# Probabilities copied by SyncE and turned as float32r, the largest transfers issued by GpSimd, in an encoder block with attention and routed experts

## The reference, cut to what matters

```python
def one_block(qblk):                      # 128 queries against all 512 keys
    sc = jnp.einsum('bqkgd,bskd->bkgqs', qblk, k).astype(jnp.float32) * scale
    p = jax.nn.softmax(sc, axis=-1).astype(v.dtype)
    return jnp.einsum('bkgqs,bskd->bqkgd', p, v)
...
o = jnp.concatenate([rms_norm(oa, p['out_norm_a']), rms_norm(ob, p['out_norm_b'])], axis=-1)
x = x + jnp.einsum('bse,ed->bsd', o, p['w_o'])
h2 = rms_norm(x, p['norm_ffn'])
x = x + expert_choice_moe(h2, p['w_router'], p['w_gate'], p['w_up'], p['w_down'])
```

## Time and profile before

| | us |
|---|---|
| median of three runs | 1082.65 (1082.18 to 1087.85) |
| the profiled execution, its own time | 1086.1 |
| its span, first to last instruction | 1083.7 |
| mean granted TensorE clock | 0.986 |
| TensorE busy | 1044.8 (96%) |
| VectorE busy | 886.0 (82%) |
| ScalarE busy | 775.3 (72%) |
| GpSimd busy | 423.3 (39%) |

### The profile page before, as it was taken

One profiled execution on the slowest core, in us unless ns is written; L12 is line 12 of the kernel. 1 busy time (PEld: TensorE's weight loads), 2 busy tenths in 40 slices (PEclk: granted clock), 3 DMA queues, 4 the chain that ended last, 5 costly groups with the idle time before them and its releaser, 6 DMA issues.

```text
span 1083.7 us, 16970 instructions
## 1 busy us (share of the span) xinstructions
PE 1044.8 (96%) x5689; PEld 896.7 (83%) x5689; DVE 886.0 (82%) x1147; ACT 775.3 (72%) x1095; POOL 423.3 (39%) x394
## 2 busy tenths in 40 slices
PE   8999999999999999998699999999999999999995
PEld 7999978999889987887578888888888888888884
DVE  6787669989999843338899999999999999999991
ACT  7655569888998843344577877877878878788771
POOL 2466576111358502334524432344323444234101
PEclk9999999999999999999799999999999999999998
DMA  8232050010211348741799999999999999999982
GB/s 305 79 116 102 1 197 1 2 41 20 98 41 40 98 109 263 225 164 79 235 417 378 398 400 400 400 421 400 401 400 400 413 408 401 400 400 406 415 310 39
DMA packets 77936, 266.05 MB, mean 245 GB/s; under 512 B 11249, under 2 KB 13516, under 8 KB 77628
## 3 DMA queue, kind: packets, MB, share of 16 engines
q1 hardware_dynamic: 69776, 239.68, 56.9%
q0 software_dynamic: 8048, 25.68, 8.3%
q10 hardware_dynamic: 60, 0.01, 0.0%
HBM read 239.07 MB, written 26.28 MB: 245 GB/s over the span
## 4 chain that ended last, share of the span: by engine, by line
PE 48%; DVE 2%; DMA 1%; issue 1%; ACT 0%; POOLq 0%; POOL 0%; DVEq 0%; ACTq 0%
PE ps L2003 10%; PE ps L2005 10%; PE ps L2004 10%; PE ps L2017 5%; PE ps L2019 5%; PE ps L2018 5%; PE ps L1980 1%; DMA xe<-h,idxT 1%; DMA out<-y,give 1%; DVE lo L2171 0%; DVE idx L1776 0%; DVE affT L1785 0%; DVE gates L1771 0%; ACT hi L2093 0%; POOLq L2274 0%
## 5 line engine op out<-in xcount | busy, mean ns | idle before, releaser
L2171 DVE TENSOR_TENSOR lo<-raw,hi 128x2048 fp32r<-128x2048 f32 x191 | 430.0, 2285 | 32.3 <-ACT hi L2093 32.0
L2093 ACT ACTIVATE hi<-raw 128x2048 fp32r<-128x2048 f32 x192 | 364.6, 1918 | 70.0 <-PE ps L2005 57.3
L2003 PE MATMUL ps<-hi,xehi 128*128 128x512 f32 x480 | 188.3, 392 | 1.3 <-DVE h L2193 1.0
L2005 PE MATMUL ps<-hi,xelo 128*128 128x512 f32 x480 | 186.9, 389 | 0.0
L2004 PE MATMUL ps<-lo,xehi 128*128 128x512 f32 x480 | 186.8, 389 | 0.0
L1939 POOL DMA_INDIRECT xe<-h,take x60 | 111.1, 1851 | 25.1 <-issue 13.7
L2003 PEld LDWEIGHTS ps<-hi,xehi 128*128 128x128 f32 x480 | 90.1, 188 | 20.2 <-issue 1.4
L2005 PEld LDWEIGHTS ps<-hi,xelo 128*128 128x128 f32 x480 | 90.1, 188 | 18.8
L2004 PEld LDWEIGHTS ps<-lo,xehi 128*128 128x128 f32 x480 | 90.2, 188 | 18.1
L1934 POOL COPY take<-idx 128x4 uint32 (+1 forms) x15 | 29.0, 1930 | 193.7 <-DVE xt L2187 187.4
L1361 DVE TENSOR_TENSOR probTlo<-ps,probThi 128x512 fp32r<-128x512 f32 x128 | 87.8, 686 | 12.1 <-ACT probThi L1318 10.0
(11 more groups left out here) (302 smaller groups left out, 2192.3 us busy)
## 6 DMA issues: line engine op xcount, KB each, us to landing
raw<-in_w_down SPq DMA_DIRECT2D x64, 1024.0 KB, 10.0
raw<-in_w_gate SPq DMA_DIRECT2D x60, 1024.0 KB, 9.7
raw<-in_w_up SPq DMA_DIRECT2D x60, 1024.0 KB, 9.3
w_raw<-in_w_in SPq DMA_DIRECT2D x8, 592.0 KB, 9.0
x<-in_x SPq DMA_DIRECT2D x8, 512.0 KB, 3.7
woraw<-in_w_o SPq DMA_DIRECT2D x4, 1024.0 KB, 5.1
o<-attention_out SPq DMA_DIRECT2D x8, 512.0 KB, 4.4
xr<-in_x SPq DMA_DIRECT2D x8, 512.0 KB, 7.0
```

What stands on the lines that cost most here:

```text
L2003: pe.matmul(ps[:, dst[n], :], rowhi[:, c, :], hi[w][:, cols], start=c == 0, stop=False)
L2005: last = pe.matmul(ps[:, dst[n], :], rowlo[:, c, :], hi[w][:, cols], start=False, stop=c == KD - 1)
L2093: act.activation(hi[s][:], raw[s][:], ACT.Copy).then_inc(hi_done, 1)
L2171: dve.tensor_tensor(lo[s][:], raw[s][:], hi[s][:].bitcast(F32), ALU.subtract).then_inc(lo_done, 1)
```

## The change

From the seventh unit on (`DIRECT = 6`), SyncE copies each unit's probabilities by DMA, SBUF to SBUF, 256 KB each, into one of three new tiles `turn`, when the exponential is done and the turns of three units ago are too. The turns read the copy. They are float32 for u % 4 = 0 and float32r for the other three of four units (and float32 for the first six units); in- and output are the same bytes seen as the other type, and the identity is written as float32r. An exponential now waits for the copy that read its buffer three units ago. All steps of attention behind the exponential come one step later (9 instead of 8 steps of drain); pairs of value products now fall on odd steps, and in them the four turns stand one by one ahead of the four "lo" products. The stores of finished heads and the loads of `w_o` are issued by GpSimd, at fixed places of its loop over key heads; SyncE issues the first row block's heads after unit 94's copy, its residual after the loop, and then what it issued before, without the stores. Some buffers change place.

```diff
@@ attend: names @@
-    STEPS = 8
+    STEPS = 9
+    turn = att["turn"]
+    turn_loaded = project_signals["w_loaded"][0:len(turn)]
+    DIRECT = 6
+    def loaded(v):
+        return turn_loaded[v % 3], 16 * (v // 3)
+    def exp_read(v):
+        return (pt_ready, v + 1) if v < DIRECT else loaded(v)
@@ attend: SyncE @@
     def sync_program(sp, route_first, route_second, route_rest):
-        for h0, h1 in O_PARTS:
-            store_heads(0, h0, h1)
-        sp.wait_ge(o_stored, 16 * len(O_PARTS))
-        for i in range(KD // 2):
-            if i >= 2:
-                sp.wait_ge(wo_lo, 2 * (i - 1))
-            sp.dma_start(wo["raw"][:, 2 * (i % 2):2 * (i % 2) + 2, :],
-                         a["w_o"].rearrange("(k p) n -> p k n", p=P)[:, 2 * i:2 * i + 2, :]).then_inc(wo_loaded, 16)
-        route_first(sp)
-        for h0, h1 in O_PARTS[:-1]:
-            store_heads(1, h0, h1)
+        for v in range(DIRECT, NU):
+            sp.wait_ge(exp_done, v + 1)
+            sp.wait_ge(pt_ready, v - 2)
+            sp.dma_start(turn[v % 3][:], att["p"][v % 3][:]).then_inc(turn_loaded[v % 3], 16)
+            if v == NU // 2 + 30:
+                route_first(sp)
         route_second(sp)
-        store_heads(1, *O_PARTS[-1])
         route_rest(sp)
@@ attend: GpSimd @@
+        stores = {QH + 5: (0, 0), HEADS: (0, 1), HEADS + GROUP: (0, 2), HEADS + QH + 4: (1, 0), HEADS + QH + 6: (1, 1)}
...
+            if g in stores:
+                s, part = stores[g]
+                store_heads(pool, s, *O_PARTS[part])
+                if (s, part) == (0, len(O_PARTS) - 1):
+                    pool.wait_ge(o_stored, 16 * len(O_PARTS))
+                    load_output_weights(0)
+                    load_output_weights(1)
             for i in split_after.get(g, ()):
                 split_output_weights(pool, i)
+                if i in (1, 3):
+                    load_output_weights((i + 3) // 2)
+        store_heads(pool, SETS - 1, *O_PARTS[-1])
@@ attend: TensorE @@
         def transpose_prob(u, i):
             if i == 0:
-                pe.wait_ge(exp_done, u + 1)
+                if u < DIRECT:
+                    pe.wait_ge(exp_done, u + 1)
+                else:
+                    pe.wait_ge(*loaded(u))
...
-            turned = pe.transpose(ps[:, T_BANKS[u % 2], cols], att["p"][u % 3][:, cols], k["ident"][:])
+            rows = att["p"] if u < DIRECT else turn
+            as_type = F32 if u < DIRECT or u % TS == 0 else F32R
+            turned = pe.transpose(ps[:, T_BANKS[u % 2], cols].bitcast(as_type), rows[u % 3][:, cols].bitcast(as_type),
+                                  k["ident"][:].bitcast(as_type))
...
-        def values(m):
+        def values(m, between):
...
                 else:
+                    if between is not None:
+                        transpose_prob(between, i)
                     pe.matmul(ps[0:VD, OT_BANK, cols], v[:, i, 0, :], ptlo[m % 2][:, i, :], start=False, stop=False)
...
-            pair = (u - 6) // 2 if u >= 6 and u % 2 == 0 and (u - 6) // 2 < PAIRS else None
-            turned = u - 3 if 0 <= u - 3 < NU else None
-            output = (u - 11) // TS if u >= 11 and (u - 11) % TS == 0 else None
+            pair = (u - 7) // 2 if u >= 7 and u % 2 == 1 and (u - 7) // 2 < PAIRS else None
+            turned = u - 4 if 0 <= u - 4 < NU else None
+            output = (u - 12) // TS if u >= 12 and (u - 12) % TS == 0 else None
@@ attend: ScalarE (and VectorE's steps, each one later in the same way) @@
                 if v >= 3:
-                    act.wait_ge(pt_ready, v - 2)
+                    act.wait_ge(*exp_read(v - 3))
...
-            if 0 <= u - 3 < NU:
-                v = u - 3
+            if 0 <= u - 4 < NU:
+                v = u - 4
@@ route: SyncE @@
     def sync_first(sp):
-        sp.wait_ge(wo_lo, KD)
-        load_rows(sp, 0)
+        sp.wait_ge(o_stored, 16 * len(O_PARTS))
+        load_attended(sp, 0)
     def sync_second(sp):
+        sp.wait_ge(wo_lo, KD)
+        load_residual(sp, 0)
         sp.wait_ge(score_ready, UNITS)
         load_rows(sp, 1)
```

More of the change, by code:

```diff
@@ L252, in build @@
         att["ot"] = bm("ot", [P, SEQ])
+        att["turn"] = [bm("turn0", [P, SEQ])]
         assert bm.at <= w_in_end, (bm.at, w_in_end)
@@ L262, in build @@
         wo["small"] = om("smallo", [P, 128])
-        wo["wr"] = om("wr", [P, KD, EXPERTS])
         wo["aff"] = [om(f"aff{i}", [P, 64]) for i in range(2)]
+        att["turn"] += [om(f"turn{i}", [P, SEQ]) for i in (1, 2)]
         assert om.at <= end
         om3 = Map(temps_at)
-        wo["o"], wo["x"] = [om2("o0", [P, D])], [om2("xr0", [P, D])]
+        om2.at += D * 4
+        wo["x"] = [om2("xr0", [P, D])]
         wo["othi"], wo["otlo"] = [om2("othi0", [P, KD, P], F32R)], [om2("otlo0", [P, KD, P], F32R)]
@@ L274, in build @@
         assert om2.at <= w_in_end
+        wo["o"] = [None]
         for i in (1, 2):
@@ L280, in build @@
         wo["gffn"] = om3("gffn", [P, D])
+        wo["wr"] = om3("wr", [P, KD, EXPERTS])
+        wo["o"][0] = om3("o0", [P, D])
         assert om3.at <= weights_at, (om3.at - weights_at)
@@ L474, in gpsimd_program @@
         steps.wait()
-        pool.affine_select(out=k["ident"][:], in_=k["ident"][:], compare_op=ALU.not_equal, fill=1.0,
+        pool.affine_select(out=k["ident"][:].bitcast(F32R), in_=k["ident"][:], compare_op=ALU.not_equal, fill=1.0,
                            base=0, pattern=[[-1, P]], channel_multiplier=1).then_inc(ident_ready, 1)
@@ L1112, in split_output_weights, with load_output_weights @@
             pool.tensor_tensor(wo["lo"][:, i, :], raw, wo["hi"][:, i, :].bitcast(F32), ALU.subtract).then_inc(wo_lo, 1)
+        def load_output_weights(i):
+            if i >= 2:
+                pool.wait_ge(wo_lo, 2 * (i - 1))
+            pool.dma_start(wo["raw"][:, 2 * (i % 2):2 * (i % 2) + 2, :],
+                           a["w_o"].rearrange("(k p) n -> p k n", p=P)[:, 2 * i:2 * i + 2, :]).then_inc(wo_loaded, 16)
+        stores = {QH + 5: (0, 0), HEADS: (0, 1), HEADS + GROUP: (0, 2), HEADS + QH + 4: (1, 0), HEADS + QH + 6: (1, 1)}
         split_after = {HEADS + GROUP: (0, 1), HEADS + QH: (2, 3), HEADS + QH + 1: (4,), HEADS + QH + 2: (5,),
@@ L1239, in tensor_program @@
                 scores(u)
-            pair = (u - 6) // 2 if u >= 6 and u % 2 == 0 and (u - 6) // 2 < PAIRS else None
-            turned = u - 3 if 0 <= u - 3 < NU else None
-            output = (u - 11) // TS if u >= 11 and (u - 11) % TS == 0 else None
-            for i in range(TS):
-                if output is not None:
-                    turn_output(output, i)
-                if turned is not None:
-                    transpose_prob(turned, i)
-            if pair is not None:
-                values(pair)
+            pair = (u - 7) // 2 if u >= 7 and u % 2 == 1 and (u - 7) // 2 < PAIRS else None
+            turned = u - 4 if 0 <= u - 4 < NU else None
+            output = (u - 12) // TS if u >= 12 and (u - 12) % TS == 0 else None
+            if pair is not None:
+                values(pair, turned)
+            else:
+                for i in range(TS):
+                    if output is not None:
+                        turn_output(output, i)
+                    if turned is not None:
+                        transpose_prob(turned, i)
             if u == NU - 3:
@@ L1295, in scalar_program @@
         for u in range(NU + STEPS):
-            if u >= 9 and (u - 9) % TS == 0:
-                g = (u - 9) // TS
+            if u >= 10 and (u - 10) % TS == 0:
+                g = (u - 10) // TS
                 act.wait_ge(pv_done, TS // 2 * (g + 1))
@@ L1356, in vector_program @@
         for u in range(NU + STEPS):
-            if 0 <= u - 4 < NU:
-                v = u - 4
+            if 0 <= u - 5 < NU:
+                v = u - 5
                 dve.wait_ge(pthi_done, v + 1)
@@ L1368, in vector_program @@
                 prepare(kind, g)
-            if u >= 11 and (u - 11) % TS == 0:
-                g = (u - 11) // TS
+            if u >= 12 and (u - 12) % TS == 0:
+                g = (u - 12) // TS
                 h = g % HEADS
```

27 lines of the change are left out of this document (16 added, 11 removed).

## The result

| | before | after |
|---|---|---|
| median of the runs | 1083.67 us (20 runs, 1082.10 to 1087.85) | 1090.98 us (20 runs, 1085.35 to 1097.54) |
| ratio, 95% interval | | 1.0063 (1.0049 to 1.0078) |
| profiled execution, span | 1086.1, 1083.7 | 1090.85, 1088.5 |
| last maximum of attention starts | 381.13 | 388.53 |
| first product of the experts starts | 531.42 | 536.05 |

What follows compares the result with a forecast made beforehand. TensorE alone was taken to bound the latent heads, with VectorE right behind at 96% in the grouped heads. Terms -5.9 - 3.3 + 1.0 + 1.3 - 3.7 = -10.6 us took the profiled 1086.1 to 1075.5, median 1072.0; range 1065 to 1083.

Steps and rivals of the forecast that it cites:

- step 7: Attention: copies that meet a 0.5 or 1 MB transfer are late, +1.0 us, bounds 0 and 8.
- Steps 1, 2 and 4: TensorE, latent heads: interleaved turns save 0.40 us a group, lone turns lose 0.02; over 16 groups -5.9 us.
- step 1: Odd units' turns between "lo" products: a pair takes 0.17 us against 0.225, saving 0.40 us a group.
- rival 2: Float32r turns load as quickly as float32 turns: another 0.2 us a latent group, -3.2, giving 1069; chance 0.12.
- Step 5: Grouped heads: VectorE at 96% leaves at most 4%; 14 settled groups at 0.24 us, -3.3.
- Step 6: SyncE's 256 KB copies: 2.3 us plus 0.3 for semaphores, hidden under 3.6 us of cover with 1 to spare.
- rival 3: The copy becomes the bound, TensorE waiting ahead of each unit's first turn; +12, 1095 us; chance 0.15.
- Step 8: Drain of attention: the last turns wait for the last copy to land, +1.3 us (0.5 to 2.5).
- Step 9: GpSimd's stream takes six stores and four loads; the work queued behind has slack, so it costs nothing.
- Step 10: After attention: earlier small loads remove TensorE's wait for the third row block and its lower clock, 2.2 + 1.5 = -3.7 us.
- steps 1 to 4: TensorE's savings in latent heads, with u % 4 = 0 staying float32 for nothing: 0.37 us a group, -5.9 in all.

Runs made afterwards that it cites:

- E1: Changed kernel with its four w_o loads cut to 32 of 1024 columns, the output product using other weights: 1076.06 us, ratio 0.9930 to the kernel before.
- E4: Changed kernel with every turn as float32, copies and all else kept: 1097.91 us, ratio 1.0130 to the kernel before.
- E7: E1's kernel with all four turns of a unit ahead of the pair's products in the grouped heads: 1076.28 us, ratio 0.9926 to the kernel before.
- E9: Changed kernel with w_o loads still issued by GpSimd, but held until units 74, 78, 91 and 101, as in E5: 1085.29 us, ratio 1.0021.
- E12: E11's kernel with five more units (53, 54, 66, 67, 118, at the stores) turned straight from the probabilities: 1078.21 us, ratio 0.9953.
- E6: Changed kernel with each 1 MB w_o load as four 256 KB pieces by SyncE, two behind each of two copies: 1082.37 us, ratio 0.9987.
- E10: E5's kernel with the turns of units with u % 4 = 0 as float32r too: 1082.54 us, ratio 1.0005 to the kernel before.
- E13: Kernel before with only the small loads (norm_ffn, router's weights) issued ahead of the last heads' store: 1082.44 us beside 1083.64, ratio 0.9988.
- E16: E13's kernel, unchanged, profiled for one more execution: 1082.30 us.
- E8: Changed kernel without any copy, all turns float32 straight from the probabilities, which get a fourth buffer: 1081.59 us, ratio 0.9983 to the kernel before.
- E3: Changed kernel with the four whole w_o loads issued by SyncE behind the copies of units 78, 82, 98 and 107: 1090.69 us, ratio 1.0073.
- E5: Changed kernel with the four whole w_o loads issued by SyncE behind the copies of units 74, 78, 91 and 101: 1081.94 us, ratio 0.9984.
- E17: Changed kernel, unchanged, profiled for a second execution: 1084.55 us beside one execution of the kernel before of 1083.97.
- E11: E5's kernel with sixteen units beside the loads turned as float32 straight from the probabilities, no copy, fourth buffer: 1077.37 us, ratio 0.9949.
- E14: Kernel before, unchanged, profiled a second time, one execution: 1090.19 us.
- E15: Kernel before, unchanged, profiled a third time, one execution: 1083.41 us.

## Why the prediction was wrong

The sum said −10.6; the medians say +7.3. The step that failed is step 7: copies that meet a big transfer were put at +1.0 us, and they cost 14.9. By its steps:

- **Steps 1, 2 and 4**, right in size, and the reason of the load wrong. −5.9 was taken. Without the loads (E1) the latent heads take 116.6 us, summed from the maximum of their first unit to that of the unit behind them or to the last maximum, and 122.6 before: −6.0. Against the change E4 gives 6.9, grouped heads and the late copies' shares included. The load of a float32r turn was taken at some 107 ns of the array's time by the float32r products' rows, and it costs what a float32 turn's does (142 ns in the view, 0.07 from turn to turn). The pair came to 0.18 where 0.17 was taken, a figure that step 1 had for either load. The lone turns gained (0.45 in all against 0.60) where 0.02 a group was to be lost: rival 2 had the load right. That the sum of these steps fits so closely is in part luck: its terms for the lone turns had the wrong sign, and a settled latent group gained 0.42 for 0.37.
- **Step 5** failed too. −3.3 was taken for grouped heads, on VectorE's idle 4%. By the same reading they take 108.1 us in E1 for 108.4 before, −0.3. That VectorE was at its bound already at 96% fits this and is argued; E7 shows only that TensorE's order is not what holds these heads.
- **Step 6** right: 2.2 us for a copy alone, and a cover of 3.75. Eleven profiles of kernels with float32r turns show the second number in one grouped group, by unit 13's copy: where it took 2.2 to 3.75 us the group took 6.24 or 6.25, where it took 3.99, 4.07, 4.25, 4.38, 4.41 and 4.43 the group took 6.49, 6.56, 6.75, 6.88, 6.91 and 6.91 (the change, E9, E12, E6, E1, E10), all of what is over 3.75.
- **Step 7** is the step that turned the sign: +1.0 taken, upper bound 8, measured 14.9 (E1). Its reasoning, "a copy behind a whole 1 MB would be 2 to 4 us late", was near: beside one load the worst copies of the change take 5.9 and 8.1 us and not 2.2. Two things were missed. It counted one or two copies late for each MB and took the first microsecond of each as covered, since "ordinary service is in turns"; in fact three in a row are late in the change, and the units chain (the exponential waits for the copy's source too, 10.0 us), so what is over the cover is paid in full. And behind the waits TensorE's clock falls (0.50 from 292 to 296 us), so that a pair takes 0.32 us for 0.18. The chance for the slower side was put on rival 3, a copy that is slow in every unit; what happened is rival 3's mechanism, at three places.
- **Step 8**, the drain: from the last maximum to the experts 147.5 and 146.5 us in the two profiles of the change, 146.6 and 146.3 in E13 and E16 without it: 0 to 1 for 1.3.
- **Step 9** right in the change as it is: E8, with the same stream of GpSimd, loses nothing. E3 shows the slack's end: one late load there, 12 us.
- **Step 10**, the mechanism right and the size one execution's. The stall goes in the change as in E13, but is worth 1.2 us, not 3.7. The profiled execution stood 3.4 above the median, and part of that was this very stall with its fallen clock. The forecast took it out once as the edit's gain and once more in going from 1075.5 to 1072.0. The last heads' store from GpSimd landed after 3.2 us in the change, so neither the 8.8 nor the 2.5 us more that this step set beside its 4.5 came.

With the measured sizes: −6.0 (steps 1 to 4), −0.3 (step 5), +0.5 (drain) and −1.2 (stall) make −7.0 without loads, where E1 has −6.3 by the medians and −7.6 by its ratio (−10.5 to −4.6). The loads' +14.4 by the ratios makes +7.4, for +6.8 by the ratio and +7.3 by the medians. What is left is less than these runs can tell.

Not every late copy has a load or a store beside it. No big transfer runs beside unit 13's copy; in each of the ten profiles in which it took over 3.4 us, one packet of 16 KB of the queue that the profile calls instruction, 0.9 to 1.8 us long, started while it ran, and where that packet came at the copy's end or behind it (E7, E5) the copy took 2.2. That one such packet on one of 16 engines holds up a copy is read from this, and no run took it away.

The rule cited in step 7 (the Trainium skill, "DMA: Bandwidth & Descriptors", "Issuing engines are not separate DMA queues"), that DMAs of all issuers share the 16 engines and interleave, agrees with E9: with the loads in GpSimd's queue and the copies in SyncE's the copies are late all the same, up to 7.8 us. The queue is not free, some 4 us beside the 6 that E5 loses against E1. The rule was read as if interleaving kept a small transfer quick. From 282.4 to 291.5 us a packet of the loads took 64.5% of 16 times 9.1 us by 506, 0.186 us, and one of the copies 0.077. An estimate from these: a 1 MB load is some 264 such packets, 16 or 17 on each engine, 3.1 us. A copy of 2.2 us that waits for one whole load would take 5.3, for two 8.3; measured are 5.9 beside the third load and 8.1 beside the first two, though 8.1 beside the fourth alone as well (5.9 in E17), and 3.3 at most behind the two loads after which no copy was issued for 2.5 us (E3, E5). The same page of the Trainium skill says, under "Queues, rings and completion order", that an engine turns from queue to queue by whole packets of some 9 to 17 descriptors; that would make such a load's share on an engine about one turn, and fits most of these numbers (what the profile counts as a packet, 3.97 KB here, would be one descriptor). It is argued and not shown: no run tried it by itself, and the 8.1 beside one load stays open.

## What to carry to other kernels

A small transfer put on the path of every step must be priced at its worst neighbour, not alone: list every big transfer that runs in the same time, add its whole time on the engines to the small one's as a first estimate (beside one load it gave 5.3 us here, and 2.7 to 8.1 were measured), and compare that with the cover. Where it doesn't fit, another queue for the big one does not cure it (E5, E9); let the steps beside it do without the small one (E11). And when the profiled execution stands above the median, look first whether the stall you mean to remove is what puts it there.

## What the runs showed of the hardware

- Float32r turns load their weights in 142 ns like float32 ones, while float32r products of the same shape take 188; four in a row take 0.45 us against 0.60.
- A copy of 256 KB within SBUF takes 2.2 us alone, up to 4.7 beside a store of finished heads (E1), and up to 8.3 beside 1 MB loads (E17).
- Float32r turns between float32 products that stream 64 columns cost more than float32 turns there: the output turns go from 253 to 273 ns on average and a latent group from 7.60 and 7.13 to 7.67 and 7.22 us (E10).
- A 1 MB load issued by GpSimd takes 5.8 to 6.5 us where SyncE's takes 5.0 to 6.7 at the same places (E9, E5) and 4.7 to 5.5 with no copies beside it (E11).
- A wait of 2.1 to 2.2 us was followed by half clock for a few microseconds in one execution (granted clock 0.72, then 1.00) and for longer in another (0.65, then 0.81 on average); one of 1.42 us by none (E14, E15). From the last maximum to the experts the two differ by 6.3 us.
